# Row exchange of the rotary turns in the mixers: four products on TensorE a layer, or eight SBUF to SBUF transfers from ScalarE's queue

## What is computed

```python
def apply_rope(x, cos, sin):
    x1, x2 = jnp.split(x, 2, axis=-1)
    c = cos[None, :, None, :].astype(x.dtype)
    s = sin[None, :, None, :].astype(x.dtype)
    return jnp.concatenate([x1 * c - x2 * s, x2 * c + x1 * s], axis=-1)

q = apply_rope(q.reshape(bsz, s_len, NSA_HEADS, dk), cos, sin) * (dk ** -0.5)
kc = compress_block(rope_k(k_cmp), kpos, kw1, kw2)
ks_blocks = rope_k(k_sel).reshape(bsz, n_slc, SEL_BLOCK, dk)
kw = jnp.pad(rope_k(k_win), win_pad)
```

## Time and profile before

| what | value |
|---|---|
| median of 3 runs | 2290.31 us (2289.16 to 2290.59) |
| the profiled execution, its own time | 2288.82 us |
| its span in the trace | 2287.0 us |
| PE busy | 2267.6 us (99% of the span) |
| DVE busy | 1697.3 us (74%) |
| ACT busy | 950.1 us (42%) |
| POOL busy | 122.9 us (5%) |
| granted clock of TensorE | 0.999 of full speed over the span |
| the layer-0 stretch of the input projection | 16 to 73 us |
| the layer-1 stretch | 336 to 390 us |

### The profile page before, as it was taken

How to read it: one execution, slowest core, us unless ns; L and a number is a source line. 1 busy time by engine, 2 the same in 40 slices (tenths; PEclk the granted TensorE clock), 3 DMA queues, 4 the chain that set the end, 5 groups by cost and what they waited for, 6 DMA issues and landing times.

```text
span 2287.0 us, 35250 instructions
## 1 busy us (share of the span) xinstructions
PE 2267.6 (99%) x14406; PEld 2014.3 (88%) x14406; DVE 1697.3 (74%) x2772; ACT 950.1 (42%) x1414; POOL 122.9 (5%) x85
## 2 busy tenths in 40 slices
PE   9999999999999999999999999999999999999998
PEld 9899999899998888898789888888888888989997
DVE  7989889989889858754546983884884673797775
ACT  6766645766542122235553212223321222475443
POOL 0110010200100000010001000001000001001001
PEclk9999999999999999999999999999999999999999
DMA  7355475355545545532111553553454453304543
GB/s 281 132 193 187 163 253 193 123 191 192 193 147 208 182 147 187 183 111 83 43 69 56 204 197 105 184 180 115 157 193 157 138 180 102 135 37 148 184 154 124
DMA packets 67025, 355.08 MB, mean 155 GB/s; under 512 B 7344, under 2 KB 10544, under 8 KB 43056
## 3 DMA queue, kind: packets, MB, share of 16 engines
q1 hardware_dynamic: 66304, 352.49, 44.4%
q10 hardware_dynamic: 560, 0.33, 0.0%
HBM read 351.75 MB, written 1.05 MB: 154 GB/s over the span
## 4 chain that ended last, share of the span: by engine, by line
PE 91%; DVE 6%; ACT 2%; issue 0%; DMA 0%; DVEq 0%; ACTq 0%
PE bank L567 90%; DVE sb_w_lo L2271 2%; ACT sb_w_hi L1498 1%; PE bank L1450 1%; DVE sb_products L2305 1%; PE bank L1324 0%; ACT sb_nP L1498 0%; DVE sb_products_up L2323 0%; DMA sb_res<-x 0%; DVE sb_decays L3014 0%; DVE sb_mid L2912 0%; ACT sb_decays L1498 0%; DVE sb_nP L3002 0%; DVE sb_mid L2883 0%; DVE sb_latP L3139 0%
## 5 line engine op out<-in xcount | busy, mean ns | idle before, releaser
L1498 ACT ACTIVATE sb_w_hi<-sb_raw 128x2048 fp32r<-128x2048 f32 (+5 forms) x301 | 491.3, 1634 | 395.6 <-PE bank L567 388.7
L2271 DVE TENSOR_TENSOR sb_w_lo<-sb_raw,sb_w_hi 128x2048 fp32r<-128x2048 f32 (+3 forms) x280 | 563.9, 2014 | 117.5 <-ACT sb_w_hi L1498 112.7
L567 PE MATMUL bank<-sb_f_pair,sb_w_hi 128*128 128x256 f32 (+1 forms) x2090 | 522.6, 339 | 1.5 <-DVE sb_w_lo L2271 1.2
L567 PE MATMUL bank<-sb_h_hi,sb_w_hi 128*128 128x512 f32 (+1 forms) x1400 | 510.8, 365 | 0.6 <-DVE sb_w_lo L2271 0.4
L567 PE MATMUL bank<-sb_h_lo,sb_w_hi 128*128 128x512 f32 (+1 forms) x1400 | 507.3, 362 | 0.0
L567 PE MATMUL bank<-sb_h_hi,sb_w_lo 128*128 128x512 f32 (+1 forms) x1400 | 507.2, 362 | 0.0
L567 PEld LDWEIGHTS bank<-sb_f_pair,sb_w_hi 128*128 128x128 f32 x2090 | 360.2, 190 | 46.5 <-DVE sb_w_lo L2271 3.5
L2305 DVE CUSTOM_DVE_ANT_0 sb_products<-sb_raw,sb_cond,sb_params 128x1024 f32<-128x1024 f32 x276 | 354.8, 1285 | 32.1 <-DVEq L2307 16.2
L567 PE MATMUL bank<-sb_f_pair,sb_w_lo 128*128 128x256 f32 (+1 forms) x1122 | 365.9, 326 | 0.0
L567 PEld LDWEIGHTS bank<-sb_h_hi,sb_w_hi 128*128 128x128 f32 x1400 | 264.1, 189 | 43.0 <-issue 0.9
L567 PEld LDWEIGHTS bank<-sb_h_lo,sb_w_hi 128*128 128x128 f32 x1400 | 264.2, 189 | 41.2 <-issue 0.5
(11 more groups left out here) (330 smaller groups left out, 2926.9 us busy)
## 6 DMA issues: line engine op xcount, KB each, us to landing
sb_raw<-w_mod SPq DMA_DIRECT2D x144, 512.0 KB, 3.2
sb_raw<-w_l_up SPq DMA_DIRECT2D x44, 1024.0 KB, 4.8
sb_raw<-w_l_in SPq DMA_DIRECT2D x22, 1024.0 KB, 6.8
sb_raw<-w_l_down SPq DMA_DIRECT2D x32, 704.0 KB, 4.7
sb_raw<-w_m0a_up SPq DMA_DIRECT2D x22, 1024.0 KB, 4.8
sb_raw<-w_m0b_up SPq DMA_DIRECT2D x22, 1024.0 KB, 4.8
sb_raw<-w_m1a_up SPq DMA_DIRECT2D x22, 1024.0 KB, 4.8
sb_raw<-w_m1b_up SPq DMA_DIRECT2D x22, 1024.0 KB, 4.8
```

The costliest lines, as they stand in the source:

```text
L567: return nc.tensor.matmul(out, lhsT, rhs, start=start, stop=stop, skip_group_check=True)
L1498: return nc.scalar.activation(out, in_, func, **kw)
L2271: V.tensor_tensor(split_part(*at, w_lo[s]), landed_part(*at, raw[raw_slot(*at)]), split_part(*at, w_hi[s]).bitcast(F32), ALU.subtract).the ...
```

## The change

In each layer, the four products with `rot`, their wait and their semaphore are taken away. ACT, behind its evacuation of panel 1, waits until that evacuation is written and issues four transfers from U to krq[:, 0:2]; behind the evacuation of panel 2 it does the same for the queries, to krq[:, 2:4]. Each transfer moves 32 partitions of 2 x 256 float32 (64 KB). DVE's `keys` and `queries` wait for the landing of their four, each on a semaphore of its own, and read the exchanged rows from krq in place of PSUM.

```diff
+        def swapped_rows(queue, out, x, sem):
+
+            for to in range(4):
+                a, b = slice(32 * to, 32 * to + 32), slice(32 * (to ^ 1), 32 * (to ^ 1) + 32)
+                queue.dma_start(out(a), x(b)).then_inc(S(sem), 16)
...
                 in_steps(50, 56)
                 pe.wait_ge(S("consts_in"), 16)
-                pe.wait_ge(S("in_evac"), e + 3)
-                for i, t in enumerate((U_KCVC, U_KS, U_Q, U_Q + 1)):
-                    last = mm(bank[2 + i // 2][:, (i % 2) * T:(i % 2 + 1) * T], con("rot"), U[:, t, PAD:UW], True, True)
-                last.then_inc(S("rotated"), 1)
                 in_steps(56, 64)
...
                     last.then_inc(S("in_evac"), 1)
+                    if j in (1, 2):
+                        act.wait_ge(S("in_evac"), e + j + 1)
+                        to = 2 * j - 2
+                        swapped_rows(act, lambda rows: krq[rows, to:to + 2, :],
+                                     lambda rows: U[rows, U_KCVC:U_KS + 1:2, PAD:UW] if j == 1 else U[rows, U_Q:U_Q + 2, PAD:UW],
+                                     f"in_swapped{j}")
...
-                def turned(x, bank_at):
-                    r = bank[bank_at][:, :].rearrange("p (a t) -> p a t", a=2)
+                def turned(x, at):
+                    r = krq[:, at:at + 2, :]
...
                 def queries():
-                    rs, xs = turned(U[:, U_Q:U_Q + 2, PAD:UW], 3)
+                    dve.wait_ge(S("in_swapped2"), 64 * (l + 1))
+                    rs, xs = turned(U[:, U_Q:U_Q + 2, PAD:UW], 2)
                     link(V.tensor_tensor(krq[:, 2:4, :], rs, xs, ALU.add))
 
                 def keys():
 
-                    dve.wait_ge(S("rotated"), l + 1)
-                    rs, xs = turned(U[:, U_KCVC:U_KS + 1:2, PAD:UW], 2)
+                    dve.wait_ge(S("in_swapped1"), 64 * (l + 1))
+                    rs, xs = turned(U[:, U_KCVC:U_KS + 1:2, PAD:UW], 0)
...
-            dve.wait_ge(S("rotated"), LAYERS + 1)
+            dve.wait_ge(S("rotated"), 1)
```

## The result

The changed kernel takes **2295.0 us**, the median of 11 executions (2294.06 to 2296.08); the kernel before, on the same chip, took 2290.0 (2289.07 to 2290.59, 11 executions). The ratio is 1.0022 with an interval of 1.0015 to 1.003: slower by 5.0 us, which is small but has its sign beyond doubt, as the whole interval lies above 1. The forecast was +1.9 us, within 0.2%; +5.0 (0.22%) lies just outside that bound, and inside the range.

The account below looks back on a forecast made before the run. PE was taken as the bound, 91% of the chain, otherwise waiting for panels' parts. Net of the products saved, layer 0 +1.12 and layer 1 +0.73 gave +1.85 us: 2290.31 + 1.85 = 2292.2 us, range 2288.7 to 2296.0.

Parts of the forecast that it names:

- The products' worth: Removing four products a layer from PE's path: 1.73 us per layer, 3.46 us in all, the most the change can bring.
- Rival 3: Issues on ACT nearly free: high 3 not late, layer 1 held by low 4; sum -2.5 us, 2287.8 us; chance 0.05.
- The path: ACT's issues delay high 3 and 4, low 3 and 4, then PE: layer 0 1.12 us longer, layer 1 0.73.
- I take 0.53, since queue and shape agree.: Price of one transfer issue on ACT's queue, 0.53 us, from two issues in a row; bounds 0.33 and 0.65.
- rival 1: Dearer issues on ACT's queue: decides from 0.76 us an issue; at 1.0 us +7.5, 2297.8 us; chance 0.08.
- the forecast's formula: Total for both layers at issue cost i: 1.85 + 12 x (i - 0.53) us, layer 0 paying twice, layer 1 once.
- The handover "0.05": Time taken for each handover between engines, or from an engine to itself: 0.05 us.
- I cost them nothing in clock: PE stalls of 1 to 1.6 us between busy stretches were taken not to lower TensorE's granted clock: 0 us.
- Landing and loads: Transfers land before DVE's keys, 14.4 and 13.2 us behind their first issue, and SP's loads stay in time: no cost.
- rival 2: Serial landing: four transfers land one after another at 5.1 us each, keys wait; +12.8 us, 2303.1 us; chance 0.03.
- an issue between 0.33 and 0.65: The forecast case for ACT's issue price in us: sums from -0.5 to +3.3 us around +1.85; chance 0.82.
- the upper end: Top of the predicted range for the whole kernel, 2296.0 us, from an issue at 0.85 us, +5.7.

Follow-up runs that it names:

- The repeat: The changed kernel itself run again, unaltered, beside the runs with two and eight issues a set: 2295.13 us, ratio 1.0022 to the kernel before.
- the filler: Changed kernel with eight idle 128x128 products put in front of step 48 of layer 1, where PE stands still: 2294.76 us, ratio 1.002.

## Why the prediction was right in kind and short in size

Its steps, beside the trace. ("High 3" and "low 4" are ACT's and DVE's parts of the panels.) The column "shifted" is the forecast moved by what the trace was late before the layer began: 0.25 us in layer 0, 3.31 in layer 1.

| start of | forecast | shifted | measured | later by |
|---|---|---|---|---|
| high 3, layer 0 | 25.27 | 25.52 | 26.05 | 0.53 |
| step 48 | 29.54 | 29.79 | 30.35 | 0.56 |
| high 4 | 33.31 | 33.56 | 34.88 | 1.32 |
| low 4 | 35.27 | 35.52 | 37.30 | 1.78 |
| step 64 | 37.61 | 37.86 | 39.64 | 1.78 |
| low 5 | 40.62 | 40.87 | 42.66 | 1.79 |
| spread_condition(3) | 45.74 | 45.99 | 47.86 | 1.87 |
| high 3, layer 1 | 345.21 | 348.52 | 349.33 | 0.81 |
| step 48 | 349.50 | 352.81 | 353.63 | 0.82 |
| low 4 | 354.01 | 357.32 | 358.13 | 0.81 |
| step 64 | 356.35 | 359.66 | 360.97 | 1.31 |

- **The products' worth** (3.46 us at most, 2.5 with free issues) was right: 2.6 by the run without the exchange, 2.7 with SP's queue. Rival 3's sum, -2.5, described a kernel that was not this one, but that exists.
- **The path** was right: ACT's issues, high 3 and high 4, low 3 and low 4, PE; layer 0 pays twice, layer 1 once. The stalls of steps 48 and 64 of layer 0, spread_condition(3) and step 48 of layer 1 are where the forecast has them; it lacks the one at spread_condition(2), and its stall at step 64 of layer 1 is not there.
- **The failed step is the term "I take 0.53, since queue and shape agree."** On this path twelve issues took 2.74 us (23.31 to 26.05), 2.95 (31.93 to 34.88) and 2.95 (346.38 to 349.33), 8.64 in all, 0.72 each. That is above the forecast's own upper bound of 0.65 and below the 0.76 of rival 1; by the forecast's formula it is +4.1 in place of +1.85. In the table it is 0.53, then 1.32, in layer 0 and 0.81 in layer 1, so 2.1 us of the 3.1 that were missing. The 0.72 is a mean of two things. From an issue to the next start on ACT it is mostly 0.62 to 0.71 us (mean 0.66), and one step in each set is longer: the first of layer 0 at 0.75, the last of the second set at 1.03 (33.85 to 34.88), and in layer 1 the step to the fourth issue at 0.94:

```profile
347.68 0.62 ACTq L495
...
348.62 0.61 ACTq L495
```

The repeat has the long steps at the same three places (0.75, 0.98, 0.94), so they are no scatter, and what makes them was not found. Nor did "queue and shape agree": the row that was taken has 128 partitions and DRAM as source, the transfers have 32 partitions and SBUF, and one pair at the start of the run stood for twelve in the middle of it. ACT's own load is not what makes the common step dear, as SP's queue has 0.60 for these issues beside 0.33 for its 1 MB loads in the same trace. Source and shape were not told apart.
- **The handover "0.05"** held for low 3 (26.05 + 1.91 = 27.96 to 28.00) and in layer 1. Between high 4 and low 4 of layer 0 it was 0.51 (36.79 to 37.30), 0.46 more than taken.
- **"I cost them nothing in clock"** was wrong by 0.4 to 0.5 us in layer 1: 1.31 against 0.81 in the last two rows, and 0.49 at step 64 (0.41 at high 6) given back by the filler.
- **The sum redone:** 1.85 + 2.13 + 0.46 + 0.50 = 4.9 us, against 5.0 measured. Each of the three errors was small; all had the same sign.
- **Landing and loads** cost nothing, as forecast: DVE's first multiplication of keys (sb_ropet, 39.50) follows low 4 without idle time. The view of the changed kernel's issues:

```profile
L495 ACTq DMA_DIRECT2D sb_mid<-sb_mid x16: 592/618/931, 23.3 to 354.4; - x16
...
DMA to landing us min/median/max: 2.3/4.0/8.6
```

The last transfer of the keys' set in layer 0, issued at 25.34, was the slowest of all; it landed 8.6 us later, 10.6 us behind the first issue, where rival 2 needed 14.4. The Trainium skill's rule ("DMA: Bandwidth & Descriptors", "Rules for kernel authors") that transfers to disjoint halves serialize is not borne out in this case at this size, if it is read as landings one after the other: four in a row at 5.1 would be 20.4 us. How the four share the transfer engines, these traces do not show.

**The chances.** The case "an issue between 0.33 and 0.65" had 0.82 and missed by 0.07 us an issue. Between its end (+3.3) and rival 1's point (+4.6) lay a gap with no case of its own, and a second and a third error of half a microsecond carried the result across it. By the bound of 0.2%, "same" had 0.87 and "slower" 0.11, and slower came, by 0.4 us and without rival 1 or 2. That +5.0 still lies inside the range is owed to the upper end, which was drawn half way into rival 1 and not by these errors. A sum in which one price is multiplied by twelve should have had its bound from more than three rows.

**What stays open.** The 0.5 us between the end of high 4 and the start of low 4 in layer 0 appear in the changed kernel, in the repeat (36.59 to 37.09), with two issues (33.80 to 34.30) and with the sets moved later (32.44 to 32.94), always where DVE is idle and waits there; at low 3, where it is idle and waits too, the handover is 0.04; the trace puts it down to "issue". What DVE does in it was not found, and no run was made for it. Nor is it settled why the clock falls behind 2.00 and 2.02 us of standing still and not behind 2.05 in the kernel with layer 1 alone, or what makes one issue in each set longer.

## What to carry to other kernels

A transfer's issue is work of the engine whose queue it is on, and it runs in program order with that engine's compute: before moving work "to DMA", count issues times the price that this case shows, 0.6 to 0.7 us on ACT and SP and 0.5 to 0.6 on POOL, and look what stands behind them on that engine. Issue from an engine that has nothing urgent behind (SP here, 2.7 us faster than before, where the same transfers from ACT are 5.0 slower), or behind the work that others wait for. Where a term is multiplied, take its bound from several rows of the same kind, and give the gap between two cases a chance of its own.

## What the hardware showed that was not expected

- An SBUF to SBUF issue of 32 partitions from ACT's queue lasts 0.59 to 0.93 us (median 0.62; the repeat has one of 1.04) and with the gap 0.72 on this path; from SP's queue 0.60; from POOL's 0.53. Halving its bytes did not make it cheaper (median 0.61, 0.65 from start to start in the first set).
- After a PE stall of 2.02 us the granted clock stood at 0.57 over the next 4 us (0.58 in the repeat, 0.61 behind 2.00 us with the products put back); after one of 1.85 us it did not fall, after one of 2.05 in another kernel not either. With eight idle products in the stall it stayed up, in the one execution that was profiled.
- Work on PE that would lie beside a wait at the 2.4 GHz level is on the path at 1.2 GHz: the four products put back cost 1.5 us, where a wait for low 4 had been expected to cover most of them.
